# The recurrent branch of a two-block transformer kernel normalised during its last units, with other edits of the same step: token slots of 512 columns, late loads on SyncE's queue, and no weight rounding on GpSimd

## The reference, cut to what matters

```python
# first block: adaptive modulation from c, then attention and a wide MLP
mod = silu(c) @ w_ada + b_ada                    # 1024 x 6144
h = rmsnorm(x) * (1 + sc1) + sh1
y = [moba_attention(8 heads), swa_attention(8 heads)](h @ w_in) @ w_out
x = x + g1 * rmsnorm(y)
x = x + g2 * rmsnorm(square(relu(h2 @ w1 + b1)) @ w2 + b2)      # 1024 -> 4096 -> 1024
# second block
z = rms_norm(x) @ w_in_2
y_a = (normalise_per_head(mlstm(z)) * norm_g * sigmoid(o)) @ w_up_a   # recurrent branch, 4 heads of 128
y_b = (rms_per_head(diff_attention(z)) * norm_g * 0.8) @ w_up_b       # 4 heads of 128
x = x + (sigmoid(z_gate_a) * y_a + sigmoid(z_gate_b) * y_b) @ w_out_2
h2 = rms_norm(x)
# 16 experts, each takes its 32 best tokens: 3 matrices of 1024 x 2048 per expert, 403 MB in all
x = x + expert_choice_ffn(h2)
out = rms_norm(x)
```

## Time and profile before

| what | value |
|---|---|
| median of 3 runs | 1527.29 us (1526.12 to 1528.37) |
| the profiled execution, its own time | 1527.02 us |
| its span, first to last instruction | 1524.7 us |
| mean granted TensorE clock | 0.88 |
| busy: PE, DVE, ACT, POOL | 1114.1, 401.8, 315.5, 54.9 us |
| moved by DMA | 516.42 MB, of which 403 MB are expert weights |
| chain that ended last, by engine | DMA 52%, PE 39%, DVE 4% |

### The profile page before, as it was taken

One profiled execution on the slowest core, in us unless ns is written; L12 is line 12 of the kernel. 1 busy time (PEld: TensorE's weight loads), 2 busy tenths in 40 slices (PEclk: granted clock), 3 DMA queues, 4 the chain that ended last, 5 costly groups with the idle time before them and its releaser, 6 DMA issues.

```text
span 1524.7 us, 17121 instructions
## 1 busy us (share of the span) xinstructions
PE 1114.1 (73%) x7544; PEld 674.8 (44%) x7544; DVE 401.8 (26%) x729; ACT 315.5 (21%) x541; POOL 54.9 (4%) x50
## 2 busy tenths in 40 slices
PE   6889999998999879965656656667555557555555
PEld 4866898987999778511122111113111113111111
DVE  2447664655768664200000000000000000000001
ACT  3246553544645544000000000000000000000001
POOL 0020000000014300000000000000000000000000
PEclk9999999999999989987888887878778889788787
DMA  9989456552763247899999999999999999999996
GB/s 366 293 282 376 136 177 194 192 192 69 221 230 119 84 193 303 371 438 428 429 435 428 434 432 429 433 430 432 429 431 432 430 435 426 434 432 426 437 428 264
DMA packets 87619, 516.42 MB, mean 339 GB/s; under 512 B 6415, under 2 KB 63226, under 8 KB 71802
## 3 DMA queue, kind: packets, MB, share of 16 engines
q1 hardware_dynamic: 82512, 508.57, 82.1%
q10 hardware_dynamic: 4106, 4.57, 0.9%
q0 software_dynamic: 928, 2.20, 0.6%
HBM read 514.12 MB, written 1.07 MB: 338 GB/s over the span
## 4 chain that ended last, share of the span: by engine, by line
DMA 52%; PE 39%; DVE 4%; issue 2%; ACT 1%; POOL 1%; ACTq 1%; SPq 0%; DVEq 0%; POOLq 0%
DMA expert_ring<-in_w_up_e 19%; DMA expert_ring<-in_w_gate_e 17%; DMA expert_ring<-in_w_down_e 15%; PE PS L517 8%; PE PS L518 8%; PE PS L519 8%; PE PS L976 5%; PE PS L1007 2%; DMA ring<-in_w_ada 2%; PE PS L511 1%; DVE wR L367 1%; PE PS L595 1%; PE PS L950 1%; PE PS L563 1%; POOL arena L1922 1%
## 5 line engine op out<-in xcount | busy, mean ns | idle before, releaser
L976 PE MATMUL PS<-expert_ring,xeT 128*32 128x512 f32 x2048 | 320.5, 784 | 234.3 <-DMA expert_ring<-in_w_up_e 126.6
L976 PEld LDWEIGHTS PS<-expert_ring,xeT 128*32 128x32 f32 x2048 | 76.3, 139 | 475.6 <-issue 217.3
L1552 DVE TENSOR_TENSOR expert_rows<-expert_rows,PS 128x512 f32<-128x512 f32 x16 | 11.0, 688 | 806.4 <-PE PS L976 806.4
L1007 PE MATMUL PS<-expert_ring,expert_rows 128*32 128x512 f32 x992 | 145.0, 739 | 90.4 <-DMA expert_ring<-in_w_down_e 88.3
L517 PE MATMUL PS<-hR,wR 128*128 128x256 f32 x632 | 183.3, 290 | 10.6 <-DVE wR L367 10.6
L359 ACT ACTIVATE wR<-ring 128x1024 fp32r<-128x1024 f32 (+2 forms) x144 | 144.3, 1051 | 216.1 <-PE PS L519 207.5
L518 PE MATMUL PS<-hR,wR 128*128 128x256 f32 x632 | 181.6, 287 | 0.0
L519 PE MATMUL PS<-hR,wR 128*128 128x256 f32 x632 | 181.5, 287 | 0.0
L367 DVE TENSOR_TENSOR wR<-ring,wR 128x1024 fp32r<-128x1024 f32 x128 | 150.8, 1221 | 105.3 <-ACT wR L359 105.2
L517 PEld LDWEIGHTS PS<-hR,wR 128*128 128x128 f32 x632 | 124.4, 197 | 12.5 <-issue 8.2
L518 PEld LDWEIGHTS PS<-hR,wR 128*128 128x128 f32 x632 | 124.3, 197 | 0.0
(11 more groups left out here) (266 smaller groups left out, 1101.2 us busy)
## 6 DMA issues: line engine op xcount, KB each, us to landing
expert_ring<-in_w_up_e SPq DMA_DIRECT2D x32, 4096.0 KB, 43.2
expert_ring<-in_w_gate_e SPq DMA_DIRECT2D x31, 4096.0 KB, 43.0
expert_ring<-in_w_down_e SPq DMA_DIRECT2D x30, 4096.0 KB, 44.4
ring<-in_w SPq DMA_DIRECT2D x32, 1024.0 KB, 5.3
ring<-in_w_in SPq DMA_DIRECT2D x31, 1024.0 KB, 6.2
ring<-in_w_ada SPq DMA_DIRECT2D x24, 1024.0 KB, 9.2
ring<-in_w_out SPq DMA_DIRECT2D x8, 1024.0 KB, 8.5
expert_ring<-in_w_gate_e SPq DMA_DIRECT2D x2, 2048.0 KB, 9.3
```

The costliest lines, as they stand in the source:

```text
L976: mm = nc.tensor.matmul(PS[32 * j:32 * j + 32, kind // 2, :], xeT[:, e // GROUP % 2, k, own], w[:, j // 2, j % 2, :, :], start=(k == 0), s ...
L1007: mm = nc.tensor.matmul(PS[32 * at:32 * at + 32, 3, :], hidT[:, c % 4, 2 * q + c // 4, :], w[c][:, 512 * half:512 * (half + 1)], start=(q ...
```

## The change

Several edits of one step. In words:

1. **Token slots.** WIN 4 and 5, all of WOUT, MIX2 4, 5, 10 to 13, and all of WOUT2 hold half of k and 512 columns instead of all of k and 256. A pair of slots fills one bank of PSUM per tile; 24 matmuls of 512 columns per slot. The copies out of PSUM follow: one engine takes tile 0, the other tile 1, both after the second slot.
2. **Late loads** go to SP's queue, in three places between slot loads (ahead of WIN+6, WIN+8 and ADA12+2).
3. **Residues** are all made by DVE in halves, those of the gate slots too. In MIX2's last step ACT copies out before it rounds.
4. **The recurrent branch** is normalised in the loop: variances at u = 4, root and factors at u = 5, centring by ACT and gating by DVE at u = 6, placing and rounding into a buffer of its own (`hA`) at u = 7. TensorE turns it ahead of half of the last gate slot. UP slots go a0, a1, b0, b1, and a0 runs before the other branch is turned. The rest of the other branch's work then has half the width.
5. **Experts' first unit** is loaded when all eight units are combined; `ahead_y` moves behind `mixed` 2.
6. **WOUT2** starts when half of the mixed sum is split, the seeding of tile 1 between its matmuls. The fourth norm takes squares by halves, the first before WOUT2's end, and scales on DVE and ACT side by side.
7. **The first gather** is made in two halves, the second after unit 0.
8. **The last unit's** second half comes in three pieces, the last 512 KB.

```diff
-BY_POOL = [g for g in SPLIT if G_GATES2 <= g < G_UP]
+MIX_TOKENS = (4, 5, 10, 11, 12, 13)
+        hA = nc.alloc_sbuf_tensor_at("hA", [P, 2, MH, S], F32R, offset=hT_at)
+        UP_BANK = (2, 0, 4, 6)
 # SP
+                if g == G_WOUT2 + 2:
+                    sp.wait_ge(unit_comb, 2 * MH)
+                    sp.dma_start(expert_ring[:, FILL[0], :], gate_up[0][0, 0]).then_inc(unit_loaded[0], 16)
+                if g == G_WIN + 6:
+                    sp.dma_start(relb[:, :], A["rel_bias"]).then_inc(consts_in, 16)
+                    sp.dma_start(const[:, P:C_END], A["shape_constants"][:, P:C_END]).then_inc(consts_in, 16)
...
+                if g == G_WIN + 8:
+                    sp.dma_start(router[:, :, :], A["w_router_2"][0].rearrange("(k p) e -> p k e", p=P)).then_inc(late_in, 16)
...
-                    sp.wait_ge(normed, 2 * TBRANCH + 2)
                 if u == 1:
-                    sp.wait_ge(act_split, 2 * TBRANCH + 2)
+                    sp.wait_ge(mixed, 2)
                     sp.dma_start(ahead_y, down[0, 1][:, 4 * D:6 * D]).then_inc(ahead_loaded, 16)
-                    sp.wait_ge(mixed, 2)
...
+                if u == EXPERTS * UNITS_EACH - 1:
+                    sp.dma_start(expert_ring[:, FILL[b], 0:4 * D], src[:, 0:4 * D]).then_inc(unit_loaded[b], 16)
+                    sp.wait_ge(pairs_used, 2 * unit_of(n - BUFFERS) + 2)
+                    for sem, first, last in zip(tail_loaded, (4, 6, 7), (6, 7, 8)):
 # TensorE
+            def tokens_half(g, half, o, t, seeded=False):
+                w = parts(g, 4)
+                for k in range(4):
+                    mm = product(o, [x[:, k, :] for x in w], [hR[:, part, 4 * half + k, t * P:(t + 1) * P] for part in range(2)],
+                                 "tokens", half == 0 and k == 0 and not seeded, half == 1 and k == 3, onto=True)
...
+            unit_turn(2 * MH - 2)
+            pe.wait_ge(unit_read, 2 * MH - 1)
+            turn_branch(0, 0)
+            pe.wait_ge(gates_out, 2 * MH - 2)
+            last_gates(0)
+            unit_values(2 * MH - 2)
+            unit_turn(2 * MH - 1)
+            last_gates(1).then_inc(slots_used, 1)
+            unit_values(2 * MH - 1)
+            pe.wait_ge(first_split, 1)
+            project(0)
+            turn_branch(1, 6)
+            pe.wait_ge(first_placed, 2)
+            project(1)
+            pe.wait_ge(act_split, 2 * TBRANCH + 2)
+            project(2)
+            project(3)
...
+            seed(0)
+            pe.wait_ge(act_split, 2 * TMIXED + 1)
+            wout2(0, 0)
+            seed(1)
+            wout2(0, 1).then_inc(slots_used, 1)
...
-            gather(0)
+            gather(0, range(KD // 2))
...
+                    if e == 0 and kind == 1:
+                        gather(0, range(KD // 2, KD))
 # VectorE, unit loop
+                if u == MH + 2:
+                    for t in range(NT):
+                        dve.wait_ge(first_centred, t + 1)
+                        V.tensor_tensor(work[:, t, 0:MW], work[:, t, 0:MW], vo[:, t, MW:2 * MW], ALU.mult).then_inc(normed, 1)
...
+                if u == 2 * MH - 1:
+                    dve.wait_ge(first_rounded, 1)
+                    V.tensor_tensor(hA[:, 1, :, :], mixT[:, 0:MH, :], hA[:, 0, :, :], ALU.subtract).then_inc(first_split, 1)
+                if u < 2 * MH:
+                    residue_slot(dve, V, G_GATES2 + u + 2)
 # ScalarE
-            late_loads()
...
-                round_slot(act, G_MIX2 + i + 2)
+                if i < N_MIX2 - 1:
+                    round_slot(act, G_MIX2 + i + 2)
...
+            round_slot(act, G_MIX2 + N_MIX2 + 1)
...
+                if u == MH + 2:
+                    act.wait_ge(factors2_set, 1)
+                    for t in range(NT):
+                        for h in range(MH):
+                            n, w = 8 * t + h, work[:, t, h * P:(h + 1) * P]
+                            last = N.activation(w, w, ACT.Identity, scale=bn6[:, n, 3:4], bias=bn6[:, n, 4:5])
+                        last.then_inc(first_centred, 1)
...
+            for t in range(NT):
+                half_square(N4, t, PS[:, 4 + 2 * t, :])
 # GpSimd
-            for g in BY_POOL:
-                residue_slot(pool, G, g)
```

More of the change, by code:

```diff
@@ L357, in round_slot @@
                 eng.wait_ge(slots_used, used(SPLIT[n - 2]))
-            for piece in pieces(g):
+            for piece in pieces():
                 nc.scalar.activation(halves(g, 0)[:, piece], slot(g)[:, piece], ACT.Copy).then_inc(slot_rounded, 1)
@@ new lines, in _ @@
+            V.tensor_scalar(b6t[:, :, 4:8, 0], mvt[:, :, 4:8, 1], EPS, None, ALU.add).then_inc(var2_set, 1)
+            dve.wait_ge(root2_set, 2)
+            then(V.reciprocal(b6t[:, :, 4:8, 3], b6t[:, :, 4:8, 2]))
+            V.tensor_scalar(b6t[:, :, 4:8, 4], b6t[:, :, 4:8, 3], 1.0 - LAM_INIT, None, ALU.mult).then_inc(factors2_set, 1)
+            dve.wait_ge(turned, 4 * TBRANCH + 3)
+            for k in range(4, KD):
+                last = V.tensor_scalar(mixT[:, k, 0:P], PS[:, 6, (k - 4) * P:(k - 3) * P], colB[:, B_DNG:B_DNG + 1], None, ALU.mult)
@@ new lines, in _ @@
+            last.then_inc(placed[0], 2)
+            for t in range(NT):
+                tile = slice(t * P, (t + 1) * P)
+                dve.wait_ge(act_rounded, 2 * TBRANCH + t + 1)
+                V.tensor_tensor(hR[:, 1, 4:8, tile], mixT[:, 4:8, tile], hR[:, 0, 4:8, tile], ALU.subtract).then_inc(act_split, 1)
+            residue_slot(dve, V, G_UP + 2)
+            hflat = hT[:, :, :].rearrange("p k s -> p (k s)")
+            yflat = mixT.rearrange("p k s -> p (k s)")
+            for i in range(N_UP):
+                br, half = i // 2, i % 2
+                part = slice(1024 * half, 1024 * (half + 1))
+                dve.wait_ge(slots_used, used(G_UP + i))
+                dve.wait_ge(gsig_set, i + 1)
+                if i == 1:
+                    dve.wait_ge(act_split, 2 * TBRANCH + 2)
+                ps = PS[:, UP_BANK[i]:UP_BANK[i] + 2, :].rearrange("p b n -> p (b n)")
+                gate = gT[:, 8 * br + 4 * half:8 * br + 4 * half + 4, :].rearrange("p k s -> p (k s)")
+                last = V.tensor_tensor((yflat[:, part], work[:, half, :])[br], ps, gate, ALU.mult)
+                if br == 1:
+                    then(last)
+                    V.tensor_tensor(hflat[:, part], yflat[:, part], work[:, half, :], ALU.add).then_inc(mixed, 1)
+                if i < 2:
+                    residue_slot(dve, V, (G_UP + 3, G_WOUT2)[i])
```

330 lines of the change are left out of this document (175 added, 155 removed).

## The result

The changed kernel takes 1504.18 us, the median of four runs (1499.71 to 1506.01), beside 1527.83 us (1526.12 to 1530.08) of the kernel before: a ratio of 0.984 with a 95% interval of 0.9814 to 0.9866. Two later comparisons of the same kernel gave 0.9829 (0.9809 to 0.9849, median 1500.89) and 0.9827 (0.9811 to 0.9843, median 1499.95).

What follows compares the result with a forecast made beforehand. TensorE's prelude up to unit 6's request, then DMA's weight stream, bound the kernel; the end moves with that request plus cuts behind the last landing. Terms sum to -27.8 us, giving 1499.5 us, range 1494 to 1509.

Steps and rivals of the forecast that it cites:

- MIX2's end to WOUT2: Unit loop and UP: earlier scores, no DVE stalls beside POOL, UP right behind the units; -13.3 us, bounds -16.5 to -7.
- Late loads: Before attention: without these loads on ACT, TensorE skips a wait and slow matmuls, -7.0 us; +0.5 for contention with bias DMAs.
- MIX2 and the copy: MIX2 to first scores: six token slots give -1.8 us; the copy ahead of the rounding starts the scores 1.9 earlier.
- WOUT2, fourth norm: Ahead of the router: WOUT2 +0.3 us, token slots against exposed seeding; norm -1.1 by shorter squares and side-by-side scaling.
- First gather: Before unit 0: half the gather leaves the path, -3.1 us; unit 7's request comes 10 us after unit 6's, +0.5.
- Last unit: Behind the last landing: only four matmuls remain, 0.6 us, instead of 16 taking 2.46; -1.7 us.
- Free: Ahead of unit 6's request: loading unit 0 at 525 instead of 550 falls into idle DMA; the hole closes almost wholly.
- the first: Rival: the six units loaded ahead become the limit, 3 us lost, 1502.5 us; chance 0.09.
- The second: Rival: DVE becomes the unit loop's bound outright, 2 us on each of the last four turns, 1507.5 us; chance 0.14.
- The third: Rival: late loads' gain lost, as constants arrive after 51 us or POOL's bias DMAs are held up; 1506.5 us, chance 0.08.
- The fourth: Rival: better than forecast, no wait reaches the clock and DVE runs ahead; 1494 us, chance 0.06.
- The fifth: Rival: a slower weight stream; at 414 GB/s the gain is gone, at 412 the time is 1532 us; chance 0.03.

Runs made afterwards that it cites:

- Held UP: Changed kernel with the first UP slot run behind the other branch's transposes instead of ahead of them: 1509.01 us, ratio 0.9885.
- the whole last half: Changed kernel with the second half of the last unit loaded as one request, its four products waiting for all of it: 1506.84 us, ratio 0.9866.

## Why the prediction was right, and where its terms were not

The forecast was 1499.5 us with a range of 1494 to 1509; the measured median is 1504.18, and 1500.89 and 1499.95 in the two comparisons after it. The direction, the rule that the end moves with unit 6's request, and the largest term are borne out.

- **MIX2's end to WOUT2, forecast -13.3.** WOUT2's first product stands 108.9 us behind MIX2's last (447.0 to 555.91), forecast 110.1 and before 123.4; in the two later profiles it is 108.1 and 108.0. The steps are right one by one: units 4, 5 and 6 are combined at 493.1, 501.8 and 511.2 and the last values taken at 524.55, forecast 493.7, 502.5, 512.9 and 525.4 when its times are moved by the 6.8 that MIX2 ends earlier. Held UP costs 8.1, POOL's residues 4.7: both of the parts that the term was made of are real. The unit loop did become DVE's, at 8.7 and 9.4 us a turn (491.43, 500.16, 509.55) for a forecast of 8.8 and 10.4 with the branch's own work in them, and TensorE still waits 2.23 and 0.38 for it. The Trainium skill, SBUF — State Buffer, section Who interferes with whom, was the better guide of the two that the prediction weighed: the runs with and without POOL's residues agree with it (5.01 against 2.23 in TensorE's wait, 3.13 against 0.35 in the multiplication). The prediction read the Trainium skill, Perfetto Trace Analysis, section Optimizing Scalar/DVE Operations, as advice against it, since work may go from a full VectorE to other engines. The same section adds that moving work between GpSimd and VectorE might not help because they share a port. The run agrees with the addition: with the residues on GpSimd the kernel is 4.7 slower.
- **Late loads, forecast -7.0 and +0.5.** The bias row and the first logits came 6.9 earlier, the clock of 50 to 55 us is 1.00. In the two later profiles the logits came 7.9 earlier. The 0.5 for contention can't be read: the bias chain took 29.0 us before, 28.0 to 29.0 in the changed kernel's profiles, and 30.0 in that of the late loads alone. What the term lacks is behind it: TensorE now reaches attention with a wait, and the opening runs at half clock for 1 to 2 us. The prediction priced that kind of loss where a wait goes, and not where one comes.
- **WOUT, forecast -1.1.** In one of three profiles -1.4, in the others +1.3, by the clock of 132 to 138 us.
- **MIX2 and the copy, forecast -3.7.** Measured -3.0 three times. The copy gave its 1.9 (TensorE stands still for 0.78 ahead of the scores instead of 2.68); MIX2's six token slots gave 1.2 and not 1.8, though no wait for a residue shows there. MIX2 ends 6.8, 7.8 and 10.4 earlier in the three profiles, forecast 9 to 10.
- **WOUT2, fourth norm, forecast -0.8.** Measured +0.2 to -0.3. WOUT2, from the split to the last squares, gave 0.5 where +0.3 was forecast. From the last squares to the end of the scaling it is 2.4 us and was 3.0 (581.05 to 583.47, 601.56 to 604.51): 0.5 and not 1.1, since DVE is still copying the first tile's transposes (581.49 to 582.6) when the root is there. What took most of both back is no term of the sum: the router's 32 matmuls took 4.4 to 4.8 in the three profiles, with the clock at 0.57 in their stretch in the first, and 3.78 before.
- **First gather, forecast -3.1 and +0.5. This is the term that failed.** Measured 0 over both in two of three profiles, and +1.4 in the first. The step that failed is that what follows the cut keeps its length: the prediction left unit 0 as it was, but its stretch was granted 0.55 (602 to 608 us), and its products took 5.4 to 5.9 in place of 3.64. Then unit 7's request came 10.7 to 11.9 behind unit 6's, not 10, and the stream took 1.2 to 2.6 longer where I had 0.5; in the first profile that is the dip to 201 GB/s at 618 to 622. With few idle products, unit 0 at 3.64, the two terms measure -3.0 and +0.7.
- **Last unit, forecast -1.7.** Measured -2.0, by another sum: the four last matmuls take 1.05 and not 0.6, which gives 1.4; the scatter behind them is 1.8 shorter by the clock, which I didn't have, and DVE's last work comes 1.0 sooner by it; 0.4 is lost at the very end. That the total is close is luck in part.
- **Free.** "The hole closes almost wholly" was wrong: ahead of unit 6's data DMA still falls to 2 GB/s at 606 to 608 (10 at 626 to 628 before), and the 400 GB/s and more that were to be seen there were 342 and 111 from 600 to 610. Unit 0's early load isn't shown to be worth anything.

That the later medians lie within 1.4 us of the forecast is luck in part. In the last profile the gather's two terms fall 2.6 short, MIX2 0.7 and WOUT2 to the router 0.5, and the late loads and the units, better by 1.4 and 0.9, make up for most of it. Some small terms also don't follow from their own parts: the slow matmuls behind the late loads come to 2.3 by the rows (29 x 0.08) and not 2.7, WOUT2's parts give +0.5 and not +0.3, the norm's 1.0 and not 1.1, and the last unit's 1.9 and not 1.7; but for the first, which the measured 6.9 doesn't single out, they nearly cancel.

Of the rivals, the first needs a DMA that is behind, and the profile shows one that waits. The second is there in its mechanism and not at its price: DVE sets the turn, and the stretch is as forecast. The third's event was seen in part, but not for its reasons: neither the constants nor the bias chain took the late loads' gain back; some of it went to the clock. The fourth is out, since waits did reach the clock. The fifth is out, at 431 GB/s.

Open: why undoing the late loads costs 4 us more in medians than in the profiled execution, and doing them alone 1 less; and why the whole last half costs 6.9 where 2.5 can be shown. The clock's changes from run to run are large enough for it, but no run shows that they are the cause. Open too is why the clock falls behind the half gather.

## What to carry to other kernels

When a kernel changes over from one bound to another, find the single event that starts the second part, and measure every cut by how far it moves that event: half a gather off the path bought nothing while the work behind it ran at half clock and the next request came later. Where waits shrink or move, price the clock at both levels on both sides of each wait; a few idle products inside a wait held it up, and too many gave most of it back; the medians don't settle that even the few pay. Two profiles of the same kernel, compared stage by stage, tell which terms can be trusted to a microsecond at all.

## What was unexpected of the hardware

TensorE's clock is not fixed by the program alone. Behind the same wait of 1.54 us it was 0.50 in one execution and 1.00 in the next, with 2.6 us on the whole kernel, and behind one of 1.69 it was 0.66 or 1.00, with 1.5 us. It also fell where TensorE never stood still: the router's 32 matmuls of 16 columns filled 584.58 to 589.4 us, and the clock of 586 to 594 was 0.57; in the kernel before the same matmuls took 3.78, in a stretch at 0.91 (604 to 610). Elsewhere the level does follow the program: unit 0's products took 5.29 to 5.86 in all eight profiles with half a gather and no idle products ahead of them, and 3.64 with them. And pieces of a load that land 1.24 us apart, with four matmuls behind each, kept it up for the work behind them, where one landing with 16 matmuls did not: the scatter took 1.99 in all eleven profiles with the pieces and 3.78 in all three without.
